# Expert products in native float32 on four column tiles, fed straight from thirteen weight slots, with down weights two rows to a partition

## The reference, cut to what matters

```python
def swiglu(v, wg, wu, wd):
    return (jax.nn.silu(v @ wg) * (v @ wu)) @ wd

def moe_swiglu(v, router, wg, wu, wd):
    logits = (v @ router).astype(F32)
    top_val, top_idx = lax.top_k(logits, TOP_K_EXPERTS)
    top_w = jax.nn.softmax(top_val, axis=-1)
    combine = jnp.sum(jax.nn.one_hot(top_idx, N_EXPERTS, dtype=F32) * top_w[..., None], axis=-2)
    y = jnp.zeros_like(v)
    for e in range(N_EXPERTS):
        y = y + combine[..., e:e + 1] * swiglu(v, wg[e], wu[e], wd[e])
    return y
```

## Time and profile before

| | us |
|---|---|
| median of three runs | 1567.45 (1567.03 to 1568.58) |
| the profiled execution's own time | 1568.84 |
| its span | 1567.1 |

### The profile page before, as it was taken

One profiled execution on the slowest core, in us unless ns is written; L12 is line 12 of the kernel. 1 busy time (PEld: TensorE's weight loads), 2 busy tenths in 40 slices (PEclk: granted clock), 3 DMA queues, 4 the chain that ended last, 5 costly groups with the idle time before them and its releaser, 6 DMA issues.

```text
span 1567.1 us, 20748 instructions
## 1 busy us (share of the span) xinstructions
PE 1548.3 (99%) x8098; PEld 1278.1 (82%) x8098; DVE 1253.5 (80%) x1438; ACT 999.7 (64%) x1219; POOL 63.4 (4%) x94
## 2 busy tenths in 40 slices
PE   8999999999999999999999999999999999999997
PEld 7887888888888888788878888888888888888876
DVE  5787878555566677788699999999999999999995
ACT  5656434544445556434578777777777877777774
POOL 3100000000000100000000000000000000001001
PEclk9999999999999999999999999999999999999999
DMA  8445445565555445452799999999999999999990
GB/s 294 136 146 176 147 151 195 177 197 188 185 194 161 151 153 169 145 169 98 280 371 384 385 384 373 385 377 385 384 374 387 370 386 379 386 377 376 395 355 28
DMA packets 212438, 421.31 MB, mean 269 GB/s; under 512 B 16194, under 2 KB 57972, under 8 KB 212340
## 3 DMA queue, kind: packets, MB, share of 16 engines
q1 hardware_dynamic: 207808, 407.69, 73.3%
q0 software_dynamic: 2880, 10.49, 1.7%
q10 hardware_dynamic: 1652, 1.80, 0.3%
HBM read 414.15 MB, written 5.77 MB: 268 GB/s over the span
## 4 chain that ended last, share of the span: by engine, by line
PE 95%; DVE 2%; ACT 1%; DMA 0%; POOL 0%; issue 0%; SPq 0%; POOLq 0%; DVEq 0%; ACTq 0%
PE ps L1518 29%; PE ps L1520 29%; PE ps L1519 29%; DVE wlo L939 1%; PE ps L1974 1%; PE ps L1617 1%; PE ps L1578 1%; PE ps L1764 1%; PE ps L1627 1%; DMA arena<-in_w_in 0%; PE ps L1943 0%; PE ps L1788 0%; ACT whi L587 0%; PE ps L1868 0%; PE ps L1749 0%
## 5 line engine op out<-in xcount | busy, mean ns | idle before, releaser
L939 DVE TENSOR_TENSOR wlo<-arena,whi 128x1024 fp32r<-128x1024 f32 x774 | 908.4, 1220 | 137.1 <-ACT whi L587 135.9
L587 ACT ACTIVATE whi<-arena 128x1024 fp32r<-128x1024 f32 x774 | 774.2, 1052 | 192.1 <-PE ps L1520 181.9
L1518 PE MATMUL ps<-whi,ahi 128*128 128x512 f32 (+1 forms) x2040 | 809.7, 397 | 4.2 <-DVE wlo L939 2.6
L1520 PE MATMUL ps<-wlo,ahi 128*128 128x512 f32 (+1 forms) x2040 | 796.0, 390 | 0.0
L1519 PE MATMUL ps<-whi,alo 128*128 128x512 f32 (+1 forms) x2040 | 794.7, 390 | 0.0
L1518 PEld LDWEIGHTS ps<-whi,ahi 128*128 128x128 f32 x2040 | 383.7, 188 | 85.3 <-issue 7.9
L1520 PEld LDWEIGHTS ps<-wlo,ahi 128*128 128x128 f32 x2040 | 383.3, 188 | 81.1
L1519 PEld LDWEIGHTS ps<-whi,alo 128*128 128x128 f32 x2040 | 384.2, 188 | 74.9
L939 DVE TENSOR_TENSOR alo<-ps,ahi 128x512 fp32r<-128x512 f32 (+2 forms) x93 | 62.5, 676 | 37.2 <-ACT ahi L587 34.8
L587 ACT ACTIVATE ahi<-ps 128x512 fp32r<-128x512 f32 (+2 forms) x46 | 27.3, 604 | 64.0 <-PE ps L1868 29.5
L716 ACT ACTIVATE ahi<-ps 128x512 fp32r<-128x512 f32 (+1 forms) x48 | 27.0, 563 | 49.8 <-PE ps L1974 49.8
(11 more groups left out here) (235 smaller groups left out, 721.2 us busy)
## 6 DMA issues: line engine op xcount, KB each, us to landing
arena<-in_moe_wg SPq DMA_DIRECT2D x176, 512.0 KB, 6.0
arena<-in_moe_wu SPq DMA_DIRECT2D x176, 512.0 KB, 6.4
arena<-in_moe_wd SPq DMA_DIRECT2D x176, 512.0 KB, 6.1
arena<-in_w_in SPq DMA_DIRECT2D x112, 512.0 KB, 4.5
arena<-in_w_branch SPq DMA_DIRECT2D x24, 512.0 KB, 4.5
arena<-in_dense_wg SPq DMA_DIRECT2D x22, 512.0 KB, 4.0
arena<-in_dense_wu SPq DMA_DIRECT2D x22, 512.0 KB, 5.0
arena<-in_dense_wd SPq DMA_DIRECT2D x22, 512.0 KB, 4.4
```

Source lines behind the costliest of these rows:

```text
L587: return nc.scalar.activation(dst, src, ACT.Copy)
L939: return V.tensor_tensor(dst, src, hi.bitcast(f32), ALU.subtract)
L1518: TE.matmul(o, ahi[:, sa], whi[:, sw], start=start, stop=False)
L1520: return TE.matmul(o, ahi[:, sa], wlo[:, sw], start=False, stop=stop)
```

## The change

- **Products.** In the experts the splits are gone. `narrow_products` multiplies a slab of 128 weight rows by 1024 columns (768 in the last of three stripes) with up to 96 tokens in three blocks of 32. Column tile i of the array holds 32 tokens. Tiles 0 to 2 take columns 0 to 511 for one block each while tile 3 takes the last 256 columns for two blocks; then tiles 0 to 2 take columns 512 to 767 and tile 3 the last 256 for the third block. That is 9 products. The last expert's down slabs use 12 products of 256 columns (`last_down_granule`).
- **Stripes.** Three of 1024, 1024 and 768 hidden columns; 35 granules per expert: 16 of 2 x 128 x 1024, 8 of 2 x 128 x 768 values, 11 down.
- **Down weights.** Granules 0 to 7 come as two transfers to 64 partitions each, with two neighbouring rows (8 KB) on a partition; the transposes pick even and odd hidden columns apart to match. Granules 8 to 10 are as before.
- **Turning.** Two rounds of three transposes for the first two stripes; for the third, ordinary products with parts of the identity, which also bring tile 3's rows to their place. One copy by ACT (`ffT_out`) follows each round.
- **Slots.** Seven in the arena and six where `whi` and `wlo` lie; SP waits for PE (`gemm_done`). The split of embedding granules waits for the last granule that used a ring slot (`RING_DONE`), which is number 280 of 280.
- **Other.** A store of a result is two DMAs of 0.39 MB together; gathers take 96 rows; the last result is combined in blocks, 24 products of 256 columns; silu and the product with up work on 768 values.

```diff
+WIDTHS = (1024, 1024, 768)
+MOE_ORDER = [(kind, 0, q) for kind in ("gate", "up") for q in range(4)]
...
+FREED = [4, 5, 6]
+for last in range(M0 - RAW, M0):
+    FREED += [last % RAW] + (pair_of(last % WR) if last >= M0 - WR else [])
+SLOT_OF = [FREED[m % len(FREED)] for m in range(N_MOE)]
...
             kind, j, q = MOE_ORDER[k]
             if kind == "down":
-                return wide(moe_wd[0, e, j * FS:(j + 1) * FS, :])
...
+                if j >= 8:
+                    return wide(moe_wd[0, e, j * FS:(j + 1) * FS, :])
+                return [(moe_wd[0, e, j * FS + i * P:j * FS + i * P + P, :].rearrange("(p c) f -> p (c f)", c=2), "pairs", i)
+                        for i in range(2)]
+            a, w = moe_wg if kind == "gate" else moe_wu, WIDTHS[j]
+            return [(a[0, e, (2 * q + c) * P:(2 * q + c + 1) * P, j * D:j * D + w], "cut", (c, w)) for c in range(2)]
...
+            if how == "pairs":
+                return r[64 * w:64 * w + 64, :]
...
-                    act.wait_ge(gemm_done, n - WR + 1)
+                    act.wait_ge(gemm_done, n - WR + 1 if n < M0 or n >= M0 + N_MOE + WR else M0 + RING_DONE)
...
+                    def narrow_products(first, tokens, weights, width, start, stop):
+
+                        long, short = width // 2, width // 4
+
+                        def one(i, b, o, at, n, start):
+                            return TE.matmul(o[tile_rows(i)], tokens(b), weights[:, at:at + n], start=start, stop=stop,
+                                             skip_group_check=True)
+
+                        for b in range(NB):
+                            one(b, b, bank(first, long), 0, long, start)
+                        for b in range(2):
+                            one(3, b, bank(first, short, b * short), 3 * short, short, start and b == 0)
+                        for b in range(NB):
+                            one(b, b, bank(first + 1, short), long, short, start)
+                        return one(3, 2, bank(first + 1, short), 3 * short, short, start)
...
+                    def down_granule(n, j):
+
+                        pe.wait_ge(*landed_when(n))
+                        for c in range(2):
+                            last = narrow_products(2, lambda b: ffT_block(j, c, b), raw_of(n)[:, c * D:c * D + D], D,
+                                                   j == 0 and c == 0, j == NS - 1 and c == 1)
+                        last.then_inc(gemm_done, 1)
```

More of the change, by code:

```diff
@@ L16 @@
 NE = 8
+Q = 32
+NB = 3
+CAP = NB * Q
 PLE = 256
@@ L243, in build @@
         ORDER += [("down", NS - 1, 0)]
[L246 to L255, removed]
         def moe_granule(e, k):
@@ L444, in _ @@
-            split(M0 + N_MOE - 1)
+            for m in range(N_MOE + 5):
+                slot = SLOT_OF[m]
+                if BEFORE[m] is not None:
+                    sp.wait_ge(gemm_done, M0 + BEFORE[m] + 1)
+                elif slot >= ARENA_SLOTS:
+                    ring = (slot - ARENA_SLOTS) % WR
+                    sp.wait_ge(gemm_done, max(n for n in range(M0) if n % WR == ring) + 1)
+                elif slot < RAW:
+                    split(max(n for n in range(M0) if n % RAW == slot))
+                else:
+                    sp.wait_ge(at_ready, 4 * 6)
+                for src, how, w in moe_granule(m // PER_E, m % PER_E) if m < N_MOE else granule(1, G_PLE0 + m - N_MOE):
+                    sp.dma_start(place(slot, how, w), src).then_inc(moe_landed[slot], 16)
@@ L860, in _ @@
                             n = M0 + e * PER_E + k
-                            if kind in ("gate", "both") and part == 0 and j > 0:
-                                ffT_hi(e, j - 1)
-                            if e == 0 and k == 8:
+                            if kind == "gate" and part < 2 and j > 0:
+                                ffT_out(e, j - 1, part)
+                            if e == 0 and k == 3:
                                 act.wait_ge(v_lo, NT)
@@ L866, in _ @@
                                     nc.scalar.activation(u_nat(t), u_nat(t), ACT.Copy, scale=rstd(4, t)).then_inc(v_nat, 1)
-                            if kind in ("gate", "both") and part == 1:
+                            if kind == "gate" and part == 3:
                                 act.wait_ge(gemm_done, n + 1)
-                                nc.scalar.activation(wk(SIL2, pair_width(j)), bank(0, pair_width(j)), ACT.Silu).then_inc(m_silu, 1)
-                            if k == PER_E - 3:
-                                ffT_hi(e, WIDE)
+                                nc.scalar.activation(sil, bank(0, ROW), ACT.Silu).then_inc(m_silu, 1)
+                            if kind == "down" and j in (7, 8):
+                                ffT_out(e, PAIRS - 1, j - 7)
                             if k == PER_E - 1:
@@ new lines, in combine_blocks @@
+                    def combine_blocks(some):
+                        for b in some:
+                            for t in range(NT):
+                                for i in range(4):
+                                    place = wk(XG + (t * NB + b) * P, P)[tile_rows(i)]
+                                    last = TE.matmul(bank(LAST_BANKS[i], FS, t * FS), place, wk(YM + b * FS, FS)[tile_rows(i)],
+                                                     start=b == 0 and t == 0, stop=b == NB - 1, skip_group_check=True)
+                        return last
@@ new lines, in up_granule @@
+                    def up_granule(n, q, part, first, width):
+                        pe.wait_ge(*landed_when(n))
+                        for c in range(2):
+                            x = XG + (q * KC + 2 * part + c) * CAP
+                            last = narrow_products(first, lambda b: wk(x + b * Q, Q), raw_of(n)[:, c * D:c * D + width], width,
+                                                   part == 0 and c == 0, part == 3 and c == 1)
+                        last.then_inc(gemm_done, 1)
```

434 lines of the change are left out of this document (241 added, 193 removed).

## The result

The changed kernel takes **1817.05 us** (median of 4 runs, 1805.83 to 1825.25); the kernel before, run beside it, 1567.6. The ratio is 1.1575, with a 95% interval of 1.1548 to 1.1602: 16% slower, where 1555 us and a range of 1530 to 1595 were forecast. The profiled execution took 1825.25 us.

A forecast was written before the change was run, and what follows sets the result against it. PE, busy 99% of the span, was taken as the bound, through the pace of its products. 1568.84 - 17.1 (experts) + 4.2 (tail) = 1555.9, given as 1555 us against the median; range 1530 to 1595.

The forecast's parts named there:

- Part 5: Expert weight transfers: at 400 GB/s an expert needs 88.5 us, less than 91.9, so they hide; half-partition bounds 205 to 411.
- Rival A: Half-partition down transfers become the bound at 205 GB/s: 108.4 us per expert, about 1660 us; chance 15%.
- Part 1: Expert products: 396 rounds of 0.2157 us, 85.4 us against 89.8, so 4.4 us less per expert.
- Rival B: Expert product rounds less dense than in the mixer, from uneven tiles and width changes: 1577 us; chance 17%.
- Part 2: Interruptions of an expert's products: seven excursions at 0.22 us plus turning, 6.5 us where before had 4.1.
- Part 3: Expert splits and waits: removed splits were hidden, copies have cover, start stays 772.2; last product's successor starts 17.1 us earlier.
- Part 4: Tail after the last expert product: splits delay the last copies, projection starts about 7.6 us after it, 4.2 us later.
- Rival C: No change: turning between products costs 8 us instead of 6.5, 12 us more, 1567 us; chance 9%.

The follow-up runs named there:

- 128-partition kernel: The changed kernel with down granules 0 to 7 fetched as two transfers over all 128 partitions, even and odd rows, 4 KB pieces: 1572.11 us, ratio 1.0025.

## Why the prediction was wrong

**Part 5 failed, and it decides the sign.** It put the unknown form between 205 and 411 GB/s and took the upper side "as every row with larger pieces is the faster one". Piece size was the wrong property: 8 KB pieces on 128 partitions change nothing (1572.8 against 1572.1), and halves cost the same with 4 KB (1829). The lower bound of 205 was sound for the halves themselves: alone they run at 205 to 262, and their packets take 37.3 us per expert in after. But it was used with the other 27.0 MB still at 400 GB/s. These took 96.7 us where 67.5 were put, so the stream behaves as if the halves ran at 126.

**Rival A was the right mechanism at too small a price.** PE waits for moe_wd, landings take three times as long, the rate falls below 300: all as it said. It gave 108.4 us per expert and 1660; it is 134.3 and 1817. Its 40.9 us for the halves were about right (37.3 of packet time); its 67.5 us for the rest were too few by 29. Its chance of 15% was too low. What stood against it, that the second half is queued at once behind the first, did not help: in after it was so queued, and the pace fell all the same.

**Part 1 was right.** Six rounds are a slab of 1.29 us, from trace to trace; 93.73 less seven interruptions of 8.45 us in all leaves 85.3 us of products for 85.4 forecast. **Rival B** thereby falls: uneven tiles and changes of width cost nothing that can be seen.

**Part 2 was mis-sized: 8.4 us for 6.5.** In the trace of the 128-partition kernel the seven are 0.79, 1.35, 0.72, 0.71, 1.35, 1.37 and 2.16, by the same subtraction (1.94 instead of 2.58 for a granule of width 768). The third pair's turning and the token products came out within 0.1. Of the 1.9 us missing, 1.2 is the wait for ACT's second copy, and most of the rest the price of leaving and entering, 0.3 to 0.4 each and not 0.22. The forecast's own rows add up to 0.30 (0.09 + 0.10 + 0.11), of which it struck a part without a row for it. The step that failed is Part 3's sentence that every copy has a granule ahead of its reader: true of the first copy of a pair, not of the second, and the wait asked for both.

**Part 3** was near on the start: PE's first expert product comes at 770.97 in the 128-partition kernel and at 774.13 in after, for 772.2. In the former the last product ends at 1521.3 and not 1507.4.

**Part 4 was 1.2 us short.** The projection starts 8.8 us after the last product, not 7.6. The combining products begin after ACT's splits and copy, 4.56 us late as worked out, but take 4.3 us where 1.7 + 0.9 were forecast from rows at full clock. The wait that the forecast itself predicted halves the clock behind it; that was left out.

**The sum, mended:** 1568.84 - 17.1 + 15.1 (8 x 1.89 for the expert) - 1.2 (start) + 4.2 + 1.2 = 1571.0, which is the profiled execution's time of the 128-partition kernel. What is left to after is Part 5's: 254 us between the two profiled executions, 245 between the medians. **Rival C**, no change through 12 us more of turning, describes the kernel without the half-partition fetch almost exactly.

## What to carry to other kernels

Before the shape of a transfer is changed, ask which partitions each single transfer touches: one that stays within partitions 0 to 63, or 64 to 127, moves at half pace, whatever its pieces, and holds up full-width transfers in the same stream, so that it costs there as much as at a third of the pace; every second partition was as good as all 128, and a range across the middle fits that too, in one run each. When a resource has a margin of 5% (88.5 of 93.7 us), an unknown form for a quarter of its bytes is the whole prediction, and its bounds deserve more care than terms of a microsecond. And for each wait, ask not whether there is cover for the data that the reader uses, but for everything that its semaphore value asks for.

## What the runs showed that was not expected

The half-partition transfers cost their neighbours more than themselves: 27 us per expert against 16, at a DMA share of 1.0 throughout. The page's busy share of the DMA engines therefore can't tell a full stream from a throttled one; only GB/s does. SP's queue takes its time over an issue as well: in after one row reads

```profile
1240.74 10.04 SPq L491 DMA_DIRECT2D arena<-in_moe_wu  x8
```

That is 1.26 us per issue, against 2.92 / 4 = 0.73 in the earlier trace rows. It stands in a stretch at full pace: the eight transfers hold 4.2 MB, 418 GB/s over these 10.04 us, where the engines moved 395 to 405. So SP issues just as fast as the engines carry away, which fits a full queue; nothing here tells whether that is the cause. And the clock fell where PE had idled: to half after the 4.56 us of the tail, and to a mean of 0.97 over after's whole span. That this added to after's loss is not shown: the DMA engines were busy all the time in the experts, and PE waited for them.
